# A hybrid GLA/MLA decoder trunk on one core: the gated linear attention taken as one sequence of items

## The reference

```python
def gla_mixer(h, w_in, w_gate2, b_gate, head_g, w_o):
    proj = h @ w_in                                   # q 1024, k 1024, v 2048, r 2048, g1 16 columns
    q, k, v, r, g1 = jnp.split(proj, [hk, 2 * hk, 2 * hk + hv, 2 * hk + 2 * hv], axis=-1)
    log_a = jax.nn.log_sigmoid((g1 @ w_gate2 + b_gate).astype(jnp.float32)) / GLA_GATE_NORM
    o = gla_chunked(q * GLA_DK ** -0.5, k, v, log_a)  # 4 heads; causal, with pairwise decays
    o = rmsnorm(o, head_g)                            # over the 512 columns of a head
    o = o * jax.nn.silu(r)
    return o.reshape(B_, S_, hv) @ w_o
```

## Time and profile before

| | us |
|---|---|
| median of 3 runs | 2476.84 |
| lowest, highest | 2469.88, 2478.08 |
| the profiled execution, its own time | 2479.71 |
| span of the profiled execution | 2478.0 |

### The profile page before, as it was taken

How to read it: one execution, slowest core, us unless ns; L and a number is a source line. 1 busy time by engine, 2 the same in 40 slices (tenths; PEclk the granted TensorE clock), 3 DMA queues, 4 the chain that set the end, 5 groups by cost and what they waited for, 6 DMA issues and landing times.

```text
span 2478.0 us, 27045 instructions
## 1 busy us (share of the span) xinstructions
PE 2358.1 (95%) x10904; PEld 1912.0 (77%) x10904; DVE 1838.5 (74%) x1731; ACT 1102.2 (44%) x1195; POOL 114.7 (5%) x145
## 2 busy tenths in 40 slices
PE   5898999899999999999999899999999999999998
PEld 2567878577887788888887688877887888878876
DVE  5766987677888887878897878787777546555565
ACT  2124443334545335543444555435565345444453
POOL 0010650000000000000000000000000000000000
PEclk8898999898999999999999899998999999999999
DMA  8955769576997997869986656685866555555554
GB/s 322 336 202 220 257 236 371 189 277 235 359 334 272 340 354 279 327 243 367 343 315 244 220 174 213 247 321 186 325 252 239 184 194 182 186 172 190 187 174 148
DMA packets 259808, 632.91 MB, mean 255 GB/s; under 512 B 23505, under 2 KB 32745, under 8 KB 233978
## 3 DMA queue, kind: packets, MB, share of 16 engines
q1 hardware_dynamic: 258842, 626.26, 70.3%
q10 hardware_dynamic: 864, 5.24, 0.5%
HBM read 629.36 MB, written 2.10 MB: 255 GB/s over the span
## 4 chain that ended last, share of the span: by engine, by line
PE 78%; DVE 8%; DMA 7%; ACT 3%; issue 3%; SPq 1%; POOL 1%; DVEq 0%; POOLq 0%; ACTq 0%
PE gm L1805 21%; PE gm L1806 21%; PE gm L1812 20%; PE tp L1846 2%; PE gm L1797 2%; DMA raw<-in_ffn_w_down_dram 2%; PE gm L1799 2%; PE gm L1798 2%; DVE w_lo L1166 2%; ACT w_hi L746 2%; DVE acc L1183 2%; DVE conv L1546 1%; DMA raw<-in_gla_w_o_dram 1%; DMA mods<-in_mod_w_dram 1%; DMA raw<-in_gla_w_in_dram 1%
## 5 line engine op out<-in xcount | busy, mean ns | idle before, releaser
L1166 DVE TENSOR_TENSOR w_lo<-raw,w_hi 128x2048 fp32r<-128x2048 f32 (+1 forms) x378 | 851.3, 2255 | 375.5 <-ACT w_hi L746 374.3
L746 ACT ACTIVATE w_hi<-raw 128x2048 fp32r<-128x2048 f32 (+1 forms) x378 | 703.6, 1863 | 740.2 <-DMA raw<-in_ffn_w_up_dram 241.0
L1805 PE MATMUL gm<-w_hi,h_hi 128*128 128x512 f32 x1816 | 726.9, 400 | 0.2 <-DVE h_lo L1245 0.2
L1806 PE MATMUL gm<-w_hi,h_lo 128*128 128x512 f32 x1816 | 715.7, 394 | 0.0
L1812 PE MATMUL gm<-w_lo,h_hi 128*128 128x512 f32 x1816 | 448.8, 389 | 0.0
L1183 DVE SCALAR_TENSOR_TENSOR acc<-mods,c_col,acc 128x2048 f32<-128x2048 f32 x180 | 422.3, 2346 | 5.2 <-DMA mods<-in_mod_w_dram 4.6
L1805 PEld LDWEIGHTS gm<-w_hi,h_hi 128*128 128x128 f32 x1816 | 346.6, 191 | 77.1 <-issue 5.0
L1806 PEld LDWEIGHTS gm<-w_hi,h_lo 128*128 128x128 f32 x1816 | 346.3, 191 | 71.3 <-issue 1.0
L1812 PEld LDWEIGHTS gm<-w_lo,h_hi 128*128 128x128 f32 x1816 | 340.8, 188 | 70.9
L1805 PE MATMUL gm<-w_hi,a_hi 128*128 128x512 f32 x692 | 279.3, 404 | 11.7 <-DVE a_lo L1569 9.6
L1806 PE MATMUL gm<-w_hi,a_lo 128*128 128x512 f32 x692 | 274.9, 397 | 0.0
(11 more groups left out here) (257 smaller groups left out, 2166.4 us busy)
## 6 DMA issues: line engine op xcount, KB each, us to landing
raw<-in_ffn_w_up_dram SPq DMA_DIRECT2D x176, 1024.0 KB, 4.9
mods<-in_mod_w_dram SPq DMA_DIRECT2D x174, 1024.0 KB, 7.2
raw<-in_ffn_w_down_dram SPq DMA_DIRECT2D x64, 1024.0 KB, 5.2
raw<-in_gla_w_in_dram SPq DMA_DIRECT2D x48, 1024.0 KB, 5.3
mods<-in_kv_mod_w_dram SPq DMA_DIRECT2D x32, 1024.0 KB, 6.9
raw<-in_ffn_w_down_dram SPq DMA_DIRECT2D x32, 768.0 KB, 4.3
pre_s<-in_mod_w_dram SPq DMA_DIRECT2D x18, 1024.0 KB, 11.1
raw<-in_gla_w_o_dram SPq DMA_DIRECT2D x16, 1024.0 KB, 9.0
```

The source lines that it names most:

```text
L746: act.activation(w_hi[:, k % RAW, 0:words], raw[:, k % RAW, 0:words], ACT.Copy).then_inc(hi_made, 1)
L1166: dve.tensor_tensor(w_lo[:, k % RAW, 0:words], raw[:, k % RAW, 0:words], w_hi[:, k % RAW, 0:words].bitcast(F32), ALU.subtract).then_inc(lo ...
L1805: pe.matmul(o, hi_s[:, kt, tok], wh[:, j, :], start=kt == 0, stop=False)
L1806: pe.matmul(o, lo_s[:, kt, tok], wh[:, j, :], start=False, stop=False)
```

## The change

The mixer's sections are reordered so that TensorE passes through k, v, r and gla_out without a stage between them.

- **k** (VectorE, ScalarE): `gate_low` and `decay_sums` stand ahead of the step's modulation and `w_lo`; the exponential and logarithm of the gate stand one step earlier on ScalarE.
- **v**: begins right behind k. The last two transposes of k follow v item 0, the diagonal follows v item 1. Units 2 to 15 shift by one step: exponents of unit n in step n+1, picking in step n+3, products after item n+2. The last two units' products fall after r items 0 and 1.
- **r**: heads 0, 1, 2 are multiplied after r items 6, 9, 12, into `ms` instead of `gm`; their squares stand in ScalarE's steps 7, 10, 13 and their gating in VectorE's steps 8, 11, 14. The reductions of groups 2 and 3 of the modulation go after items 2 to 5 and 14. ScalarE's loop over r is unrolled.
- **gla_out**: head 3 and the first two splits follow the last r item. The other six splits are dealt out, two to a step, over steps 0 to 2 of ScalarE and VectorE, ahead of the step's other work. Of the 12 modulation blocks the one at item 3 goes, so that items 4 and 5 carry two each.

```diff
-        ("mod_v", 1, 0, 0, 0, 5),
-        ("r", 2, 8, 2, 0, 0),
-        ("o", 1, 0, 0, 8, 0),
+        ("mod_v", 1, 0, 0, 0, 4),
+        ("r", 1, 16, 4, 0, 0),
+        ("o", 1, 0, 0, 8, 6),
+        ("mod_r", 1, 0, 0, 0, 1),
+        ("o3", 1, 0, 0, 0, 2),
...
-            ("gla_out", 4, 4, (3, 4, 4, 5, 6, 7, 8, 9, 10, 11, 12, 13)),
+            ("gla_out", 4, 4, (4, 4, 5, 5, 6, 7, 8, 9, 10, 11, 12, 13)),
...
+        UNIT_STEP = (0, 1) + tuple(n + 1 for n in range(2, len(UNITS)))
+        UNIT_AT = {k: n for n, k in enumerate(UNIT_STEP)}
...
-                if k == 2:
+                if k == 1:
                     act.wait_ge(z_abs, 4)
                     step.link(act.activation(la[:, :, :], la[:, :, :], ACT.Exp, scale=-1.0))
-                if k == 3:
+                if k == 2:
                     act.activation(la[:, :, :], la[:, :, :], ACT.Ln, bias=1.0).then_inc(z_log, 1)
...
+            for k in range(16):
+                if k < 15:
+                    hi(s.item + AHEAD + k)
+                factors(16 + k)
+                if k == 0:
+                    load_gate(0, 2)
+                if k in (7, 10, 13):
+                    head_squares((7, 10, 13).index(k))
+                if k in (3, 7, 11):
+                    evac(s.item + k, ch % 2, r_sb[:, :, ch * W:(ch + 1) * W], func=ACT.Silu)
+            act.wait_ge(item_used, s.item + 16)
+            o_split_hi(0)
+            o_split_hi(1)
+            evac(s.item + 15, 1, r_sb[:, :, 3 * W:4 * W], func=ACT.Silu)
+            head_squares(3)
+            hi(s.item + AHEAD + 15)
...
                 for k in range(16):
+                    if k < 3:
+                        o_split_hi(2 * k + 2)
+                        o_split_hi(2 * k + 3)
...
+                if k == 6:
+                    dve.wait_ge(la_made, TT)
                 if k in (6, 7):
                     decay_sums(2 * k - 12)
                     decay_sums(2 * k - 11)
-            turned(s, 2)
-            turned(s, 3)
+                mods_at(s.item + k)
+                lo(s.item + AHEAD + k)
...
+            def score_step(k):
+                if k == 2:
+                    dve.wait_ge(consts, 3)
+                    for hh in range(2):
+                        pick(a["diag"].ms + hh, 7, hh)
+                if 3 <= k < 19:
+                    dve.wait_ge(ms_free, a["v"].ms + k - 3)
+                    picked(k - 3)
+                if k in UNIT_AT:
+                    exponents(UNIT_AT[k])
...
+                if k == 0:
+                    turned(a["k"], 2)
+                    turned(a["k"], 3)
+                    step.link(dve.memset(st[:, :, :, :], 0.0))
...
             s = a["r"]
             for k in range(16):
+                score_step(16 + k)
+                if 3 <= k < 7:
+                    gate_row(2, k - 3)
+                if k in (8, 11, 14):
+                    gated_head((8, 11, 14).index(k))
+                if k == 15:
+                    reduced(3)
+                    o_split_lo(0)
+                    o_split_lo(1)
                 mods_at(s.item + k)
                 lo(s.item + AHEAD + k)
...
+            gated_head(3)
             dve.wait_ge(x_in, 32)
             add_section("gla_out", "norm1")
...
+                if k == 0:
+                    turn_qk(a["k"], 2)
+                    turn_qk(a["k"], 3)
+                if k == 1:
+                    pe.wait_ge(tp_free, a["k"].tp + 4)
+                    diagonal(0)
+                    diagonal(1)
+                if k >= 2:
+                    scores(k - 2)
...
+            def turn_o(kt):
+                if kt % 2 == 0:
+                    pe.wait_ge(tp_free, a["o"].tp + kt // 2 + 1)
+                elif kt // 2 < 6:
+                    turn_head(kt // 2 + 2)
...
+                if k < 2:
+                    scores(14 + k)
+                if 2 <= k < 6:
+                    reduce_mod(2, (k - 2,))
+                if k in (6, 9, 12):
+                    head_out((6, 9, 12).index(k))
+                if k == 13:
+                    turn_head(0)
+                    turn_head(1)
+                if k == 14:
+                    reduce_mod(3)
+            head_out(3)
+            section("gla_out", h_hi, h_lo, turn_o)
```

More of the change, by code:

```diff
@@ L501, in words_of, with o_fill @@
             return NARROW.get(n, ITEM) if isinstance(n, int) else ITEM
+        def o_fill(h, t):
+            return (at["o"].ms + 2 * h if h < 3 else at["o3"].ms) + t
+        UNIT_STEP = (0, 1) + tuple(n + 1 for n in range(2, len(UNITS)))
+        UNIT_AT = {k: n for n, k in enumerate(UNIT_STEP)}
         def made(fill):
@@ L1223, in mods_at, with split @@
                     mod(n, n % MODS, g, kt)
-            def split(name, count, dst, hi_of, scale, shift, from_=0, wrap=KT):
+            def split(name, count, dst, hi_of, scale, shift, from_=0, wrap=KT, both=both):
                 fill = a[name].tp
@@ L1303, in add_section @@
                 for k in range(15):
+                    if k < 3:
+                        o_split_lo(2 * k + 2)
+                        o_split_lo(2 * k + 3)
                     if k == 7:
@@ L1445, in _ @@
             for k in range(8):
-                mods_at(s.item + k)
-                lo(s.item + AHEAD + k)
                 if k in (1, 2):
@@ L1457, in _ @@
                     decay_sums(2 * k - 11)
-            turned(s, 2)
-            turned(s, 3)
-            s = a["diag"]
-            step.link(dve.memset(st[:, :, :, :], 0.0))
-            dve.wait_ge(consts, 3)
+                mods_at(s.item + k)
+                lo(s.item + AHEAD + k)
+                if k in (5, 6):
+                    turned(s, k - 5)
             def pick(fill, level, hh):
@@ L1471, in pick @@
                     ms[:, fill % 2, :].rearrange("p (k i) -> p k i", k=4)).then_inc(ms_free, 1)
-            for hh in range(2):
-                pick(s.ms + hh, 7, hh)
             def exponents(n):
@@ L1926, in body @@
                             gm_free(s.chunk + 2 * i + k // 4)
-                        turn = (lambda kt: turn_wide(turned, kt, r_sb)) if turned and k < 4 else None
+                        turn = turned if k < 4 else None
                         item(s.item + 8 * i + k, s.item + k, hi_s, lo_s, k // 4, k % 4, turn=turn,
@@ L2052, in _, with diagonal @@
                     turn_qk(s, 1)
-            turn_qk(s, 2)
-            turn_qk(s, 3)
-            pe.wait_ge(tp_free, s.tp + 4)
-            s = a["diag"]
-            for hh in range(2):
-                o = ms_open(s.ms + hh)
+            def diagonal(hh):
+                o = ms_open(a["diag"].ms + hh)
                 for hl in range(2):
@@ L2095, in _ @@
                 item(s.item + k, s.item + k, h_hi, h_lo, (k // 4) % 2, k % 4)
-                if 1 <= k < 5:
-                    reduce_mod(2, (k - 1,))
-            pe.wait_ge(ms_free, a["v"].ms + 16)
-            for h in range(HEADS):
-                if h < 2:
-                    gm_free(a["gla_out"].chunk + h)
-                else:
-                    pe.wait_ge(o_gated, h - 1)
-                v0, v1 = v_sb[:, 0, h * DV:(h + 1) * DV], v_sb[:, 1, h * DV:(h + 1) * DV]
-                pe.matmul(gm[:, h % 2, 0, :], st[:, h, 0, :], v0, start=True, stop=True)
-                pe.matmul(gm[:, h % 2, 1, :], sx[:, h, :], v0, start=True, stop=False)
-                pe.matmul(gm[:, h % 2, 1, :], st[:, h, 1, :], v1, start=False, stop=True).then_inc(o_ready, 1)
-            reduce_mod(3)
-            pe.wait_ge(o_gated, HEADS)
-            section("gla_out", h_hi, h_lo, "o")
+                if k < 2:
+                    scores(14 + k)
+                if 2 <= k < 6:
+                    reduce_mod(2, (k - 2,))
+                if k == 6:
+                    pe.wait_ge(u_made, a["v"].chunk + 4)
+                if k in (6, 9, 12):
[7 more added lines that the diff above has]
+            section("gla_out", h_hi, h_lo, turn_o)
             reduce_mod(4)
```

76 lines of the change are left out of this document (35 added, 41 removed).

## The result

| | before | after |
|---|---|---|
| median, us (runs, range) | 2475.22 (4, 2469.88 to 2478.08) | 2438.31 (4, 2437.15 to 2442.16) |
| the profiled execution's own time, us | 2479.71 | 2437.15 |
| its span, us | 2478.0 | 2435.4 |
| mean granted clock | 0.965 | 0.974 |

Before has one run more here than at the prediction, so its median is 2475.22 and not 2476.84. The ratio of after to before is 0.9866 with a 95% interval of 0.984 to 0.9893: the changed kernel is faster, by 36.9 us between the medians, and 2438.31 lies in the range. 35.8 us were forecast.

A forecast was written before the change was run, and what follows sets the result against it. TensorE, busy over nine tenths of the span, was the bound; only its idle and half-clock time could be won. 12.2 + 2.1 + 5.7 + 14.8 + 1.0 = 35.8 us off 2479.71 gave 2443.9, or 2441.0 as median; range 2429.5 to 2458.5.

The forecast's parts named there:

- k and what follows it: In k, waits for gate_low and decay_sums and their half clock go, 12.2 us; between k and v, 2.1 us.
- v: Over v's items and score units, 9.1 us are lost; the new order wins 5.7 us, bounds 0 and 9.1.
- the 3.4: In v, 3.4 us of remaining waits booked, since TensorE's and VectorE's chains end together; bounds 0 and 9.1.
- r: In r, the moved-in heads, units and reduction cause no wait; slack 5.3 us per head, cost nothing, bounds 0 and 3.
- The seam: From r to gla_out, 15.0 of 29.9 us are wait and half clock; 14.8 us come off.
- gla_out: In gla_out, 12.9 us lost before and 11.9 after: 1.0 us gained, bounds -12.9 and +10.
- The wait at kt = 4: Early in gla_out, TensorE waits 3.0 us for split 2, and loses 2.2 for the clock behind it.
- The late wait: Late in gla_out, the wait of 1.95 us and 1.9 of clock stay, plus 2.9 of DMA backlog.
- 1, the clock swings in v: In v, shifted units come up to 1 us late and half clock follows: +17.5 us, 2458.5; chance 0.10.
- 2, the seam gives little: Behind r, VectorE's queue is longer and DMA full; gla_out loses 10 us more than before: 2452; chance 0.14.
- 3, k's waits move to v item 2: In k, w_lo and modulation come later, v item 2 waits; 7 us of gain return: 2448; chance 0.09.
- 4, the heads stall VectorE: In r, late squares stall gating and weights, 12.2 us for each of four heads: +48.8, 2490; chance 0.05.

The follow-up runs named there:

- after_again: The changed kernel unchanged, measured again alongside other kernels: median 2440.42 us, ratio to before 0.9869.
- e12: The changed kernel with r's last modulation block ahead of the output's first two splits, and gla_out's 12 blocks one to an item from 1 to 12: 2432.1 us.
- e9: The changed kernel with 12 repeated VectorE subtractions, 13.7 us of work, added over v's items: 2449.24 us.
- e7: The changed kernel with one modulation block at item 3 of gla_out again and one instead of two at item 5: 2439.36 us.
- e8: The changed kernel with its 12 modulation blocks in gla_out one to an item, from item 1 to 12: 2436.63 us.
- e2: The changed kernel with decay_sums put back behind the step's modulation, w_lo and copy of k: 2445.52 us.
- e6: The changed kernel with head 3's gating and splits 2 and 3 ahead of item 2's modulation block and w_lo on VectorE: 2446.33 us.
- e10: The changed kernel with the modulation block of r's last item moved ahead of the output's first two splits on VectorE: 2439.0 us.
- e5: The changed kernel with the six dealt-out splits of the output together again, ahead of gla_out's first other work on ScalarE and VectorE: 2448.2 us.

## Why the prediction held, point by point

**k and what follows it: right.** 14.3 us (12.2 + 2.1) were booked, 15.1 measured. From the low products of item 1 to those of item 2 pass 7.58 us in after, where 12.66 passed: 5.1, with 5.3 booked. From item 6's to item 7's pass 7.24 (213.85 to 221.09), where 14.09 passed: 6.9, as booked. The other 3.1 are the step into v (2.6, with 2.1 booked) and a small wait for `u` that is gone (0.5). VectorE's copy of the decay sums ends at 213.96 and TensorE needs its room at 215.67, a lead of 1.7 us; 1 was estimated.

**v: right in sign, mis-sized.** The term was 5.7 us, 9.1 less 3.4 of remaining waits; 8.5 were gained. The step that failed is the 3.4: waits of 0.44 us are left in after (0.11 and 0.33), 0.9 to 1.0 in after_again and e12. Its reason, two chains that end together, was right (e9). What I took too dear was unit 2 (1 to 3 us late): it comes without a wait. After's last score products begin at 351.86; 352 was forecast.

**r: right in its waits, with a term missing.** Heads 0, 1 and 2 cost 0.22 us of waiting in all. The slack of 5.3 us was enough.

**The seam: right in mechanism, 2.5 us too large.** 14.8 were booked for it and nothing for r; both together gave 12.3. The first product came 2.9 us behind r (2.7 booked). What was missing is the clock behind the reduction, which now stands ahead of r's last item. PE's timeline, then windows of after:

```profile
437.42 3.70 PE L1928 MATMUL ms<-ones,acc 128*128 128x1 f32 x32
440.98 0.48 PE L1851 MATMUL gm<-w_hi,h_hi 128*128 128x512 f32 x1
...
442.02 0.63 PE L1852 MATMUL gm<-w_hi,h_lo 128*128 128x512 f32 x1
```

```profile
430.00:437.00 7.00, 7.00 (x36) 5.88 (x35) 4.45 (x3) 3.07 (x5) 1.83 (x2) 1.00 1.02 387
437.50:441.00 3.50, 3.50 (x33) 3.50 (x33) 3.50 (x3) 1.91 (x1) 0.00 (x0) 1.00 0.89 306
441.20:444.20 3.00, 3.00 (x9) 2.27 (x9) 1.27 (x2) 0.00 (x0) 0.00 (x0) 0.54 0.32 116
```

The item behind the reduction runs 1.6 us longer than its neighbour (7.34 against 5.73, from the first start to the last end), without a wait ahead of it. The other 0.9 us: 0.5 at head 0, whose item takes 8.52 us with its wait against 8.04 at heads 1 and 2, and 0.2 each around the reduction and at gla_out's first product.

**gla_out: 2.6 gained where 1.0 was booked.** Three steps of that term:
- The wait at kt = 4 was booked at 3.0 us and is 2.40. Its working was right: the modulation at 452.58, `w_lo`, then head 3, and the split ends 11.8 us behind r, as forecast.
- The 2.2 us of half clock behind it did not come: six products follow in 1.63 us, full pace. I had taken the value near a wait of 4.12 us; the lower bound, nothing, was right here. That is partly luck: in two of nine profiles with the same wait, half clock follows it (last section).
- The late wait was booked at 1.95 with 2.9 of backlog, 4.85, and is 3.43, with about 1.7 of clock behind it (from 543.34 to the reduction at 550.53, 7.19 us for an item). I gave its growth to DMA; e7 and e8 show that it follows the modulation's places, which is the load and VectorE's work in one. PE's timeline at item 15:

```profile
543.34 0.50 PE L1843 MATMUL gm<-w_hi,h_hi 128*128 128x512 f32 x1 [3.43 <-DVE w_lo L1193]
...
543.95 0.63 PE L1845 MATMUL gm<-w_hi,h_lo 128*128 128x512 f32 x1
...
550.53 3.63 PE L1928 MATMUL ms<-ones,acc 128*128 128x1 f32 x32
```

These three come out 4.4 us below what was booked, the section only 1.6: of the 10.3 us that it loses (99.48 from the first product to the reduction, less 89.2 for items and transposes), 2.8 lie in short delays of under 0.5 us each for which I had no term.

So the total is right partly because the terms' errors offset each other: +0.8, +2.8, -2.5 and +1.6 us make the 38.5 measured out of 35.8. The mechanism of each term held; that the sum came within about 1 us of the medians' difference is luck, with 26 to 40 us as the interval of the gain.

**The rivals.** 1, the clock swings in v: no, it is 1.00 over 222 to 352, in e9 with its waits too. The rule it rested on (the Trainium skill, "TensorE: Matmul & The Clock Gate", section "A second HAM failure mode: psum-queue depth-cycling") is neither shown nor refuted by that: idle times between these products were few and short. 2, the seam gives little: its mechanism is real at kt = 4, but as the 2.4 us that the forecast already held. 3, k's waits move to v item 2: no wait there. 4, the heads stall VectorE: no.

## What to carry to other kernels

Fill the wait at the end of a stage with items of the next, not by making the late chain faster: taking away the two r items between the last score products cost 10.8 to 13.5 us. Before you price a wait that goes, count the queue of each engine ahead of its releaser; at the seam ScalarE's was 1 us ahead of VectorE's, and taking 2.36 us out of the one gave only 0.85. A small reduction of one-column products is worth a look at the granted clock behind it. Whether it does better where idle time follows anyway was not tried. Don't take a gain from the profile of one execution: the half clock behind the same wait comes and goes.

## What the hardware showed that I had not expected

**Half clock without a wait.** 32 products of one column each keep TensorE busy for 3.7 us, and the clock behind them is at the lower of its two levels (1.2 GHz) for about 3 us: a window of 0.54, products 0.43 us apart instead of 0.23. The length varies between executions: eight such products in after, twelve in after_again (the item takes 8.4 us there). In the kernel before the same reduction stood ahead of the wait of 1.78 us and of a window with clock 0.52 (488 to 491), so half clock that I put down to waits there may have been the reduction's.

No run took the reduction away, but the traces hold the case many times over. Such a reduction with a product right behind it and no wait between stands at four more places behind the mixer, before and after, and at this one in twelve of the profiles: 68 times in the fourteen. In 64 of them at least six of the next products start 0.40 us or more apart, where 0.23 is full pace; in the other four, all at one place and in e2, e6, e7 and e9, none does. In after, each stretch of four or more products at half pace from the mixer on stands behind such a reduction or a wait. So the term that I missed could have been read in the trace of before. Windows behind the reduction, one of before, then of after and of e2 at the same place:

```profile
1183.80:1186.80 3.00, 3.00 (x9) 2.33 (x8) 1.61 (x2) 1.91 (x1) 0.00 (x0) 0.50 0.98 373
```

```profile
861.50:864.50 3.00, 3.00 (x9) 2.32 (x8) 2.85 (x3) 0.08 (x1) 0.00 (x0) 0.50 1.07 408
```

```profile
867.20:870.20 3.00, 3.00 (x15) 2.44 (x15) 1.82 (x2) 1.50 (x1) 0.00 (x0) 1.00 0.98 375
```

**A wait of 2.40 us without half clock.** Behind 2.40 us (after) and 1.55 us (e10) the products followed at full pace, and the window of e9 with waits up to 1.75 us has clock 1.00; behind 1.79 and 4.17 us and 3.43 us (after) they did not. The length of the wait does not decide by itself, and neither does it together with the work ahead: the wait of 2.38 to 2.41 us at kt = 4 stands in nine profiles behind the same products, and in seven of them full pace follows, while in e5 and e7 some ten matmuls behind it run at half. The wait of 3.11 to 3.45 us at item 15 has half clock behind it in eight profiles and none in e2. Windows of e7 at kt = 4 and of e2 at item 15:

```profile
463.00:466.00 3.00, 3.00 (x12) 2.48 (x11) 2.93 (x3) 0.84 (x2) 0.00 (x0) 0.60 0.47 182
```

```profile
550.00:553.00 3.00, 3.00 (x14) 2.44 (x13) 3.00 (x2) 3.00 (x6) 0.00 (x0) 1.00 0.98 362
```

So a price for the clock behind one wait is a chance and not a fixed sum, and a difference of 2 us between two profiles can be that alone.

**GpSimd held up by VectorE.** The root of head 3's sums, two elements for each partition, takes 2.80 us beside a VectorE instruction with two inputs in SBUF, and 0.69 in the kernel e10, where VectorE is idle at that time. All fourteen profiles agree: the root takes 2.80 in the nine in which VectorE's modulation block starts 0.1 us ahead of it, and 0.69 to 0.72 the other 47 times. GpSimd's timeline of after, then of e10:

```profile
452.68 2.80 POOL L682 TENSOR_TENSOR stats<-stats,half_neg 128x2 f32<-128x2 f32 x1
```

```profile
453.99 0.69 POOL L682 TENSOR_TENSOR stats<-stats,half_neg 128x2 f32<-128x2 f32 x1
```

It ends at 455.48, 0.54 us behind the end of VectorE's block (454.94), as if it began its work only then. The Trainium skill ("SBUF — State Buffer", section "Who interferes with whom") says that a VectorE instruction with two SBUF inputs contends with a GpSimd one that reads SBUF, and calls it an exclusive lock; this row agrees with it. So do rows of v, where both engines lose. GpSimd's timeline of after, then VectorE's:

```profile
345.59 2.47 POOL L722 TENSOR_TENSOR ex<-ex,qk_t 128x512 f32<-128x512 f32 x1 [1.72 <-ACT ex L920]
```

```profile
346.60 3.60 DVE L1193 TENSOR_TENSOR w_lo<-raw,w_hi 128x2048 fp32r<-128x2048 f32 x1
```

The multiplication takes 1.29 us at its shortest. Here it starts beside a modulation block of VectorE that ends at 346.68, and ends 1.4 us behind that; `w_lo`, 2.29 us alone, takes 1.3 more.
